# Spread gates stored in the order of the output stage's reads: short writes and long reads in a hybrid conv/HGRN2/PEER layer

## Chip, cores and metric

The kernel runs on one core of a Trainium2 chip. The metric is the device time of one execution in microseconds; smaller is better.

## What is computed

One decoder layer over 1024 tokens of 1024 features: a mixer (convolution and gated recurrence), then PEER, a retrieval over 128 x 128 single-neuron experts, and a final norm. The change lies in PEER:

```
s1, i1 = top_k(sc[:, :, 0], 16); s2, i2 = top_k(sc[:, :, 1], 16)     # 8 heads, 128 keys on each side
top_s, ci = top_k((s1[..., :, None] + s2[..., None, :]).reshape(t, 8, 256), 16)
experts = i1[ci // 16] * 128 + i2[ci % 16]
gate = softmax(top_s)
act = gelu(einsum('thkd,td->thk', u_tab[experts], xb))
y   = einsum('thk,thkd->td', gate * act, v_tab[experts])
h   = h + y;  out = rmsnorm(h)
```

## The kernel before

Tokens stand in 8 tiles of 128. For two of them (GATHERED) the chosen expert rows are fetched by indirect DMA and handled on VectorE. For the other six (DENSE, TD = 768 tokens) the kernel computes all 16384 experts densely: TensorE makes the activation of every expert for every token, the gates of the chosen ones are spread into a dense array that is zero elsewhere, and the product of both is multiplied with the whole value table. Experts are worked on as 128 columns of 128, an expert's place within a column being the partition.

**Activation stage** (`select_and_activate`, lines 1411 to 1980), 128 columns. For a column SP loads a 512 KB weight tile (`Ring.load`, L84), ScalarE splits it in a high part and a scaled copy (`Ring.high`, L89 and L90), GpSimd makes the low part (`Ring.low`, L95), TensorE does two units of 24 matmuls (L1605 to L1607), ScalarE applies the gelu (L1663) to `ge`, and SP writes it to `acts_dram` (L1570). Weight tiles alternate between two buffers, and SP issues the load for column s + 2 ahead of the activation write of column s (`pick`, L1566). The columns run in parts: 64 beside the top-k searches on VectorE (`pick`), 4 of lead, 48 in which the gates are spread (`spread`), 12 `alone`.

**Spreading.** For eight tokens at a time (an octet, two per column) VectorE builds one-hot matrices (L1923 to L1927), TensorE multiplies them (L1638), and ScalarE copies the result from PSUM into `tile` (two L1707 per octet). `tile` has two halves u of 32 tokens x 128 columns (16 KB a partition); a half is full after two columns, and SP then writes its 2 MB to `gates_dram` (L1578), 24 writes in all. ScalarE waits for the semaphore `g_st[u]` before it fills a half again (L1704). In `spread` ScalarE's order within a column is gelu, octet, gelu, octet, then L89 and L90 for the column after next. The rows of the weight table that the two other tiles need are fetched by GpSimd (L1758) on the software queue and used by VectorE (L1800), between the steps above.

**Output stage** (`combine`, L1983 on), 32 groups of CPG = 4 columns. SP loads a group's gates (`Head.load_gates`, L329, 1.5 MB) and activations (`Head.load_acts`, L333, 1.5 MB), and four value tiles of 512 KB (`Head.load_values`, L345); VectorE multiplies gates and activations (`weigh`, L317), ScalarE and GpSimd split values and weights (L2171, L2177; L2198, L2203), TensorE does 144 matmuls (L2152 to L2154), VectorE adds the result (L2320) and works on gathered rows (L2298) that GpSimd fetches (L2237). Gates of groups 0 and 1 come early, in the `alone` columns, in four pieces each (`Head.load_piece`, L340), after SP has waited for the last gates writes (L1589).

Each engine takes its instructions in order. SP issues all plain DMAs on one hardware queue; GpSimd issues the gathers on a software queue. Both queues run on the same 16 DMA engines.

`gates_dram` has the shape (24, 128, 4096): block b of 32 tokens, partition, and 128 columns x 32 tokens. `Head.__init__` gives the view of it by group that the reads use (L298).

Of the kernel before, what the change touches and what calls it, by code (L numbers as in the profile page):

```python
# [6 lines left out]
P = 128  # L7
# [19 lines left out]
TD = DENSE * P  # L27
DHALF = TD // 2
GT = 32
CPG = 4  # L30
GROUPS = NK // CPG
# [40 lines left out]
class Ring:  # L72
# [3 lines left out]
    def __init__(self, sems, label, buffers, base):  # L76
        self.wf, self.wh, self.wl = buffers
        self.w_in = [sems(f"{label}_in{s}") for s in range(2)]
        self.w_hi, self.w_lo = sems(f"{label}_hi"), sems(f"{label}_lo")
        self.base = base  # L80
# [204 lines left out]
class Head:  # L285
# [5 lines left out]
    def __init__(self, sems, scores, gates, acts, v_t, vf, share):  # L291
        flat = scores[:, :, :, :].rearrange("p a h n -> p (a h n)")
        size = CPG * TD
        at = flat.shape[1] - 4 * size
        self.vh = flat[:, 0:at].bitcast(BF16).rearrange("p (s c n) -> p s c n", s=2, c=CPG)
        self.gt = flat[:, at:at + 2 * size].rearrange("p (s b c t) -> p s b c t", s=2, c=CPG, t=GT)
        self.at = flat[:, at + 2 * size:at + 4 * size].rearrange("p (s c n) -> p s c n", s=2, c=CPG)
        self.gates = gates.rearrange("b p (g n) -> g p b n", g=GROUPS)  # L298
        self.acts = acts.rearrange("(g c) p n -> g p c n", g=GROUPS)
        self.v_t, self.vf = v_t, [vf[:, s, :] for s in range(2)]  # L300
        self.v_in = [sems(f"v_in{s}") for s in range(CPG)]
        self.g_in = [sems(f"gt_in{s}") for s in range(2)]
        self.a_in = [sems(f"at_in{s}") for s in range(2)]
        self.w_ok, self.w_hi, self.w_lo = (sems(n) for n in ("gw_ok", "gw_hi", "gw_lo"))


        self.ge_st = [sems(f"ge_st{s}") for s in range(2)]
        self.share = share
        self.w_first = [share[:, i * size // 2:(i + 1) * size // 2].bitcast(BF16).rearrange("p (c n) -> p c n", c=CPG)
                        for i in range(2)]  # L310
# [1094 lines left out]
def after(eng, sem, count):  # L1405

    if not (isinstance(count, int) and count <= 0):
        eng.wait_ge(sem, count)  # L1408


def select_and_activate(nc, ctx, sb, sems, psum, scores, ident, iota16, const_b, xh, xl, ring, u_t, gates, acts, rows,
# [73 lines left out]
    flat = scores[:, :, :, :].rearrange("p a h n -> p (a h n)")  # L1485
# [4 lines left out]
    tile = flat[:, at:at + 2 * NK * GT].rearrange("p (u c t) -> p u c t", u=2, c=NK)  # L1490
# [6 lines left out]
    g_st = [sems(f"g_st{s}") for s in range(2)]  # L1497
# [8 lines left out]
    def slots(eng, pick, lead, spread, between=None, unroll=None, few=None, last=None):  # L1506


        for j in range(PICK):
            pick(j, j % 2, 0, j)  # L1510
        for start, end, body in (((1, TB, pick),) if few is None else (
                (1, FEW_TURNS, few), (FEW_TURNS, ALL_TURNS, pick))):
            with eng.Fori(start, end) as n:
                for j in range(PICK):
                    body(PICK * n + j, j % 2, n, j)
        if between is not None:
            between()
        for j in range(LEAD):
            lead(PICKED + j, j % 2, j)
        for j in range(LOOP):  # L1520
            spread(FIRST_G + j, j % 2, 0, j)
        with eng.Fori(1, SPREAD // LOOP if last is None else SWITCH - 1) as n:
            for j in range(LOOP):
                spread(LOOP * n + (FIRST_G + j), j % 2, n, j)
        if last is not None:

            n = SWITCH - 1
            for j in range(LOOP):
                (spread if j < LOOP - 2 else last)(LOOP * n + (FIRST_G + j), j % 2, n, j)
            with eng.Fori(SWITCH, SPREAD // LOOP) as n:  # L1530
                for j in range(LOOP):
                    last(LOOP * n + (FIRST_G + j), j % 2, n, j)
        if unroll is not None:
            for j in range(ALONE):
                unroll(LAST_G + j, j % 2, j)
            return
        with eng.Fori(0, ALONE // LOOP - 1) as n:
            for j in range(LOOP):
                pick(LOOP * n + (LAST_G + j), j % 2, None, 2 * n + j // 2, j)
        for j in range(LOOP):  # L1540
            pick(NK - LOOP + j, j % 2, None, (ALONE - LOOP + j) // 2, j)
# [12 lines left out]
    def more(s):  # L1554

        return not (isinstance(s, int) and s >= NK - 2)

    with nc.Block() as blk:
        @blk.sync
        def _(sp):  # L1560
            def load(s, par):

                after(sp, u_lo, s - 1)
                ring.load(sp, par, u_t[ds(s, 1), :, :])

            def pick(s, par, n, j, slot=None):  # L1566
                if more(s):
                    load(s + 2, par)
                sp.wait_ge(a_ge, 2 * s + 2)
                sp.dma_start(acts[ds(s, 1), :, :].rearrange("a p n -> (a p) n"), ge[:, par, :]).then_inc(ge_st[par], 16)  # L1570

            def spread(s, par, n, j):
                pick(s, par, n, j)
                if j % 2 == 1:

                    u = j // 2
                    sp.wait_ge(g_ok, 16 * n + (8 * u + 8))
                    sp.dma_start(gates[ds(2 * n + u, 1), :, :].rearrange("a p n -> (a p) n"),  # L1578
                                 tile[:, u, :, :].rearrange("p c t -> p (c t)")).then_inc(g_st[u], 16)

            def alone(s, par, j):

                if j >= ALONE - 2:
                    sp.wait_ge(u_lo, s + 1)
                    head.load_values(sp, par, par)
                pick(s, par, None, j)
                if j == 1:
                    for u in range(2):
                        sp.wait_ge(g_st[u], 16 * (SPREAD // LOOP))  # L1589
                if 0 < j <= 2 * PIECES:  # L1590
                    head.load_piece(sp, (j - 1) // PIECES, (j - 1) % PIECES)

            sp.dma_start(xtok[0], normed[0, :, :]).then_inc(tok_in, 16)
            slots(sp, pick, lambda s, par, j: pick(s, par, None, j), spread, unroll=alone)

        @blk.tensor
# [850 lines left out]
```

## Time and profile before

| | |
|---|---|
| median of 3 runs | 2834.77 us (2832.07 to 2835.41) |
| span of the profiled execution | 2830.4 us |
| TensorE, VectorE, GpSimd, ScalarE busy | 97%, 77%, 58%, 39% of the span |
| DMA | 658.08 MB, mean 233 GB/s |
| gates writes | 24 of 2048 KB, median 9.2 us to landing |
| gates reads, activation reads | 30 each of 1536 KB, 16.4 and 19.8 us |

The trace is one execution recorded by the hardware profiler. Times are from the start of the span. PE is TensorE's matmuls, PEld its weight loads, DVE is VectorE, ACT ScalarE, POOL GpSimd, SP SyncE. PE's ends are modelled, since matmuls are pipelined. "Idle before <- X" says what ended an engine's idle time. A DMA packet is one contiguous piece; q1 is the queue of SP, q0 that of GpSimd. The DMA share is the mean busy share of the 16 DMA engines.

### The profile page before, as it was taken

How to read it: one execution, taken by the hardware profiler on the slowest of the kernel's cores; microseconds unless marked ns; L12 is line 12 of the kernel's file. 1: busy time of each engine (PE TensorE's matmuls, PEld its weight loads, DVE VectorE, ACT ScalarE, POOL GpSimd, SP SyncE). 2: the span in 40 equal slices, each digit the busy share in tenths (PEclk: the TensorE clock that was granted, in tenths of full speed). 3: DMA queues.
4: the chain of work that ended last, by engine and by line, in shares of the span. 5: the costliest groups of instructions: out<-in, count | busy, mean ns of one | idle time of the engine just before them, and what ended most of it. 6: DMA issues, size and time to landing. Idle time of an engine off the chain costs nothing. (4 is left out here: it accounts for less than half of the span.)

```text
span 2830.4 us, 47325 instructions
## 1 busy us (share of the span) xinstructions
PE 2757.7 (97%) x16000; PEld 1508.1 (53%) x16000; DVE 2169.3 (77%) x4268; ACT 1115.4 (39%) x1554; POOL 1628.8 (58%) x1485
## 2 busy tenths in 40 slices
PE   6999999999999999999999999999999999999998
PEld 3445754554666666656666665444444444444443
DVE  3998865322788999989999994777777777777778
ACT  4354554223444444446677664312211221222122
POOL 1331001111233444477777775888888898889884
PEclk9999999999999999999999999999999999999999
DMA  3231030111344555568888888899999999999995
GB/s 128 79 137 35 1 139 22 58 47 42 110 156 162 191 192 185 177 238 308 321 308 308 322 307 321 316 367 330 338 343 339 328 343 358 352 343 352 358 349 189
DMA packets 265252, 658.08 MB, mean 233 GB/s; under 512 B 17552, under 2 KB 116112, under 8 KB 261952
## 3 DMA queue, kind: packets, MB, share of 16 engines
q1 hardware_dynamic: 190992, 387.37, 38.2%
q0 software_dynamic: 74160, 269.52, 26.7%
q8 instruction: 45, 0.74, 0.1%
q14 instruction: 55, 0.45, 0.1%
HBM read 547.24 MB, written 110.10 MB: 232 GB/s over the span
## 5 line engine op out<-in xcount | busy, mean ns | idle before, releaser
L95 POOL TENSOR_TENSOR w_low<-w_ring,w_high 128x1024 f16<-128x1024 f32 x164 | 375.3, 2289 | 884.9 <-ACT w_ring L90 884.3
L1605 PE MATMUL psum<-region_y,w_high 128*128 128x384 f16 x2048 | 670.4, 327 | 10.8 <-issue 4.3
L1606 PE MATMUL psum<-region_y,w_high 128*128 128x384 f16 x2048 | 670.5, 327 | 0.0
L1607 PE MATMUL psum<-region_y,w_low 128*128 128x384 f16 x2048 | 670.4, 327 | 0.0
L2320 DVE TENSOR_TENSOR region_x<-region_x,psum 128x1024 f32<-128x1024 f32 x192 | 234.3, 1220 | 213.6 <-PE psum L2154 213.4
L2171 ACT ACTIVATE scores<-w_ring 128x1024 bf16<-128x1024 f32 x64 | 67.0, 1048 | 655.6 <-PE psum L2154 651.6
L2152 PE MATMUL psum<-scores,share 128*128 128x512 bf16 x752 | 286.0, 380 | 7.7 <-DVE region_x L2320 6.9
L2152 PE MATMUL psum<-scores,wh 128*128 128x512 bf16 x768 | 291.2, 379 | 1.4 <-POOL wl L2203 1.4
L2154 PE MATMUL psum<-scores,wl 128*128 128x512 bf16 x768 | 291.2, 379 | 0.0
L2153 PE MATMUL psum<-vl,wh 128*128 128x512 bf16 x768 | 291.2, 379 | 0.0
L1663 ACT ACTIVATE ge<-psum 128x384 f32<-128x384 f32 x256 | 124.9, 488 | 415.6 <-PE psum L1607 413.5
L2153 PE MATMUL psum<-vl,share 128*128 128x512 bf16 x752 | 285.9, 380 | 0.0
L2154 PE MATMUL psum<-scores,share 128*128 128x512 bf16 x752 | 285.9, 380 | 0.0
L1605 PEld LDWEIGHTS psum<-region_y,w_high 128*128 128x128 f16 x2048 | 200.7, 98 | 139.4 <-issue 13.8
L1607 PEld LDWEIGHTS psum<-region_y,w_low 128*128 128x128 f16 x2048 | 200.9, 98 | 134.0 <-issue 2.2
L1606 PEld LDWEIGHTS psum<-region_y,w_high 128*128 128x128 f16 x2048 | 200.8, 98 | 126.8 <-issue 2.1
L2298 DVE SCALAR_TENSOR_TENSOR psum<-region_y,weight,psum 128x1024 f32<-128x1024 f32 x176 | 226.4, 1286 | 11.3 <-DVE psum L2298 4.2
L89 ACT ACTIVATE w_high<-w_ring 128x1024 f16<-128x1024 f32 x164 | 172.8, 1054 | 86.5 <-DMA w_ring<-in_u_t_dram 66.3
L1707 ACT ACTIVATE scores<-psum 128x512 f32<-128x512 f32 x192 | 188.8, 1088 | 30.9 <-PE psum L1638 30.9
L2237 POOL DMA_INDIRECT region_y<-in_v_t_dram,step_rows x176 | 167.6, 952 | 48.7 <-issue 48.4
L90 ACT ACTIVATE w_ring<-w_ring 128x1024 f32<-128x1024 f32 x164 | 171.6, 1046 | 0.0
L1758 POOL DMA_INDIRECT scores<-in_u_rows_dram,u_step_rows x112 | 129.7, 1158 | 25.4 <-issue 18.8
(306 smaller groups left out, 5478.3 us busy)
## 6 DMA issues: line engine op xcount, KB each, us to landing
w_ring<-in_u_t_dram SPq DMA_DIRECT2D x128, 512.0 KB, 6.1
acts_dram<-ge SPq DMA_DIRECT2D x128, 384.0 KB, 4.8
gates_dram<-scores SPq DMA_DIRECT2D x24, 2048.0 KB, 9.2
scores<-gates_dram SPq DMA_DIRECT2D x30, 1536.0 KB, 16.4
scores<-acts_dram SPq DMA_DIRECT2D x30, 1536.0 KB, 19.8
w_ring<-in_v_t_dram SPq DMA_DIRECT2D x64, 512.0 KB, 11.0
more_v<-in_v_t_dram SPq DMA_DIRECT2D x64, 512.0 KB, 4.9
w_ring<-in_w_stream_dram SPq DMA_DIRECT2D x20, 512.0 KB, 3.5
```

The costliest lines, as they stand in the source:

```text
L89: act.activation(self.wh[:, s, :], self.wf[:, s, :], ACT.Copy, scale=WS)
L90: act.activation(self.wf[:, s, :], self.wf[:, s, :], ACT.Copy, scale=WS).then_inc(self.w_hi, 1)
L95: pool.tensor_tensor(self.wl[:, s, :], self.wf[:, s, :], self.wh[:, s, :], ALU.subtract).then_inc(self.w_lo, 1)
L1605: pe.matmul(a, uh[:, par, row], xh[:, n, cols], start=(n == 0), stop=False)
L1606: pe.matmul(a, uh[:, par, row], xl[:, n, cols], start=False, stop=False)
L1607: last = pe.matmul(a, ul[:, par, row], xh[:, n, cols], start=False, stop=(n == KC - 1))
L1707: act.activation(tile[:, u, :, at:at + 4].rearrange("p c t -> p t c"), psum[:, 4 + 2 * r + b, :].rearrange("p (t c) -> p t c", t=4), ACT.C ...
L2152: pe.matmul(a, wh[par][:, c, rows], vh[:, par, c, cols], start=(c == 0), stop=False)
L2153: pe.matmul(a, wh[par][:, c, rows], vl[:, par, c, cols], start=False, stop=False)
L2154: last = pe.matmul(a, wl[par][:, c, rows], vh[:, par, c, cols], start=False, stop=(c == CPG - 1))
L2298: dve.scalar_tensor_tensor(out=acc[tile], in0=row[j], scalar=weight[:, tile, ds(at, 1)], in1=acc[tile], op0=ALU.mult, op1=ALU.add).then_in ...
L2320: dve.tensor_tensor(a, a, banks, ALU.add).then_inc(y_ok, 1)
```

## The change

The array `gates_dram` keeps its size and its data; their order in it becomes group, partition, block of 32 tokens, then the group's 4 columns x 32 tokens. A group's gates of one partition are then 24 x 512 B = 12 KB in one piece. A block's gates of one partition, which were 16 KB in one piece, are now 32 pieces of 512 B, one in each group's part. The SBUF side of every transfer, all instructions, waits and the order of issues stay.

```
-        self.gates = gates.rearrange("b p (g n) -> g p b n", g=GROUPS)
+        flat = gates.rearrange("b p n -> (b p n)")
+        self.gates = flat.rearrange("(g p b n) -> g p b n", g=GROUPS, p=P, b=TD // GT)
+        self.gates_of = flat.rearrange("(g p b n) -> b p g n", g=GROUPS, p=P, b=TD // GT)
...
                     sp.wait_ge(g_ok, 16 * n + (8 * u + 8))
-                    sp.dma_start(gates[ds(2 * n + u, 1), :, :].rearrange("a p n -> (a p) n"),
-                                 tile[:, u, :, :].rearrange("p c t -> p (c t)")).then_inc(g_st[u], 16)
+                    sp.dma_start(head.gates_of[ds(2 * n + u, 1), :, :, :].rearrange("a p g n -> (a p) g n"),
+                                 tile[:, u, :, :].rearrange("p (g c) t -> p g (c t)", c=CPG)).then_inc(g_st[u], 16)
```

## Rows read from the trace of the kernel before

**Rows 1.** Busy us (x instructions) by stage; last TensorE's granted clock, DMA share, GB/s
```profile
1300.00:1700.00 400.00, 399.24 (x3318) 270.36 (x3317) 383.56 (x540) 277.95 (x334) 289.60 (x252) 1.00 0.82 312
1820.00:1900.00 80.00, 72.32 (x325) 31.91 (x324) 67.60 (x68) 20.93 (x24) 70.49 (x67) 0.96 1.01 363
1900.00:2300.00 400.00, 400.00 (x1855) 181.34 (x1854) 294.58 (x334) 88.56 (x102) 350.56 (x335) 1.00 0.96 337
2400.00:2700.00 300.00, 298.47 (x1378) 134.02 (x1377) 232.51 (x201) 64.08 (x74) 268.57 (x257) 1.00 0.98 350
```
**Rows 2.** Timeline of SP in the spread stage: start, duration, line, operation
```profile
1421.54 0.33 SPq L1578 DMA_DIRECT2D gates_dram<-scores  x1
1422.07 0.35 SPq L84 DMA_DIRECT2D w_ring<-in_u_t_dram  x1
1428.77 0.33 SPq L1570 DMA_DIRECT2D acts_dram<-ge  x1
1429.30 0.35 SPq L84 DMA_DIRECT2D w_ring<-in_u_t_dram  x1
...
1440.82 0.33 SPq L1578 DMA_DIRECT2D gates_dram<-scores  x1
...
1460.08 0.33 SPq L1578 DMA_DIRECT2D gates_dram<-scores  x1
```
**Rows 3.** Timeline of ScalarE, same turn; in brackets idle time and what ended it
```profile
1432.74 1.06 ACT L89 ACTIVATE w_high<-w_ring 128x1024 f16<-128x1024 f32 x1 [1.73 <-DMA w_ring<-in_u_t_dram]
1433.70 1.04 ACT L90 ACTIVATE w_ring<-w_ring 128x1024 f32<-128x1024 f32 x1
1434.65 0.47 ACT L1663 ACTIVATE ge<-psum 128x384 f32<-128x384 f32 x1
1435.02 1.95 ACT L1707 ACTIVATE scores<-psum 128x512 f32<-128x512 f32 x2
```
**Rows 4.** Timeline of GpSimd, same turn
```profile
1434.82 2.92 POOL L95 TENSOR_TENSOR w_low<-w_ring,w_high 128x1024 f16<-128x1024 f32 x1 [3.58 <-ACT w_ring L90]
```
**Rows 5.** Timeline of TensorE, first matmul of the next column
```profile
1438.46 0.32 PE L1605 MATMUL psum<-region_y,w_high 128*128 128x384 f16 x1
```
**Rows 6.** Waits, 1260 to 1720 us: total us, times, longest
```profile
ACT w_high L89 <- DMA w_ring<-in_u_t_dram: 44.8, 22, 3.4
...
PE psum L1605 <- POOL w_low L95: 0.8, 1, 0.8
```
**Rows 7.** DMA queues (packets, MB, share of 16 engines): 1425.5-1427.5; 1832-1838; 1886.6-1887.9; 2135.5-2136.5
```profile
q1 hardware_dynamic: 45, 0.74, 94.7%
...
q0 software_dynamic: 441, 1.58, 67.7%
q1 hardware_dynamic: 1233, 0.63, 37.6%
...
q1 hardware_dynamic: 316, 0.16, 64.9%
...
q1 hardware_dynamic: 346, 0.18, 70.4%
```
**Rows 8.** Landings: gates writes 1300-1700, gates reads 1830-2760; last, SP's L333 (ns)
```profile
DMA to landing us min/median/max: 7.4/8.9/10.3
...
DMA to landing us min/median/max: 14.9/16.4/25.3
...
L333 SPq DMA_DIRECT2D scores<-acts_dram x30: 6440/10029/19663, 1822.8 to 2728.2; - x30
```
**Rows 9.** Timeline of GpSimd, gathers issued beside the write and the load
```profile
1428.58 1.25 POOL L1758 DMA_INDIRECT tk_work<-in_u_rows_dram,u_step_rows  x1 [0.15 <-issue]
1430.14 1.10 POOL L1758 DMA_INDIRECT tk_work<-in_u_rows_dram,u_step_rows  x1 [0.31 <-issue]
```
**Rows 10.** Waits in the output stage, 1820 to 2800 us
```profile
ACT scores L2171 <- PE psum L2154: 651.6, 30, 22.5
DVE region_x L2320 <- PE psum L2154: 212.0, 151, 2.8
...
ACT scores L2171 <- DMA w_ring<-in_v_t_dram: 3.9, 1, 3.9
ACT scores L2171 <- DMA more_v<-in_v_t_dram: 3.1, 2, 2.5
```
**Rows 11.** Gates writes (count, first to last start); timeline of SP after the last
```profile
L1578 SPq DMA_DIRECT2D gates_dram<-scores x24: 332/332/343, 1267.3 to 1711.5; - x24
...
1726.36 0.34 SPq L1570 DMA_DIRECT2D acts_dram<-ge  x1
```

## Prediction, made before the changed kernel was run

> **What bounds the kernel now.** I read first the busy times by stage [rows 1]. In the spread stage (the 48 columns in which the gates are spread and written, about 1267 to 1726 us) TensorE is busy 399.2 of 400 us at full clock; in the output stage it is busy 400.0 of 400 in its first half and 298.5 of 300 in its second, with one gap of 7.7 us just after its start (1820 to 1900). So TensorE sets the time of both stages that the change touches, and nothing gained off TensorE can be worth more than its idle time. The question is only whether the change makes TensorE wait.
>
> Second view: the order of SP's issues in the spread stage [rows 2]. A turn is two columns: the gates writes start at 1421.54, 1440.82 and 1460.08, so a turn is 19.27 us, and there are 24 writes [rows 11]. Half a microsecond behind each write, on the same queue, stands the load of the weight tile that TensorE needs one and a half columns later.
>
> Third view: what happens when that load lands [rows 3 to 5]. ScalarE starts L89 at 1432.74, after an idle time of 1.73 us that the DMA ended: 11.2 us after the write was issued at 1421.54. L89 and L90 take 1.9 us, GpSimd's L95 runs from 1434.82 to 1437.74, and TensorE begins the column that needs it at 1438.46. This path has 0.7 us to spare. It is not a single case: ScalarE waited for that DMA 22 times in the stage, 44.8 us in all, while TensorE lost 0.8 us to it once [rows 6]. The load behind the gates write is the one thing in the stage that is nearly late.
>
> **The change, part by part.** (a) Each of the 24 writes keeps its 2 MB, but a partition's 16 KB row becomes 32 pieces of 512 B, 12 KB times 128 apart in memory: 4096 pieces in place of 128. (b) Each of the 30 reads keeps its 1.5 MB and has 12 KB rows in place of 24 pieces of 512 B; the 8 early pieces have 3 KB rows. (c) Nothing else moves; no instruction and no wait is added.
>
> Cost of the write in the DMA engines. With 16 KB rows, hardware-queue packets took 94.7% of 16 engines x 2 us for 45 packets: 673 ns each, so 128 / 16 x 673 ns = 5.4 us. For 512 B pieces the trace of before has only reads. Beside backlogged gathers 1233 packets took 37.6% of 96 us: 29.3 ns each; 4096 / 16 x 29.3 ns = 7.5 us is the lower end. But alone on the engines these pieces did not come at that pace: 316 in 1.3 us (243 per us) with the engines 64.9% busy, and 346 in 1.0 us at 70.4% [rows 7]. Something ahead of the engines supplied only 243 to 346 per us: 16.9 to 11.8 us for 4096. I take the middle, 295 per us, 13.9 us, since the write mostly meets engines that are not backlogged. The far end is the read's whole landing: 14.9 us at least for 3072 pieces [rows 8], by 4/3 19.9 us, against 8.9 us for a write now, so 11.0 us more.
>
> The Trainium skill (DMA: Bandwidth & Descriptors, Specifications) gives 512 B as the smallest transfer that runs at line rate. By that the write would stay as it is and this sum would be zero. The trace disagrees even in engine time alone: 512 B in 29.3 ns is 17.5 GB/s per engine, 16 KB in 673 ns is 24.3 [rows 7].
>
> The load behind it. L, from the write's issue to ScalarE's start, is now 11.2 us. It grows by 13.9 - 5.4 = 8.5 us. Against that, two gathers that now share the engines with the load (issued at 1428.58 and 1430.14 [rows 9]) will mostly be through before it: 256 packets / 16 x 147 ns (from the 441 packets of the software queue in 67.7% of 96 us [rows 7]) = 2.4 us. L = 11.2 + 8.5 - 2.4 = 17.3 us.
>
> What a turn then takes. ScalarE is in order: behind the load it must do L89 and L90, a gelu, the octet's two copies, another gelu and two copies before SP may issue the next write: 1.9 + 0.4 + 1.95 + 0.4 + 1.95 us [rows 3], with 0.1 for the semaphore 6.7 us. So a turn is the longer of 19.27 us and L + 6.7. Now: 17.9, hidden. After: 24.0, which is 4.7 us more per turn. TensorE follows: its column starts after L + 1.9 + 2.9 and stands idle for the same 4.7 us. 24 turns x 4.7 us = 113 us.
>
> Queues behind it. SP, ScalarE and GpSimd wait in order. SP: in the output stage the acts load issued right behind a 512 B gates read held SP for 6.4 to 19.7 us [rows 8], so SP will be held likewise at the weight load behind the write, and the acts write and the next column's load, now issued 7.2 and 7.8 us after the gates write [rows 2], go out later. The turn of 24 us leaves both time, so I add nothing; if not, the second column of a turn waits too (in the far end of the range). ScalarE's own wait for a tile half that is still being written: it reuses that half one turn later, and the write lands at about 8.9 + 8.5 = 17.4 us, inside 24. GpSimd's gathers behind L95 shift with the turn; VectorE is busy 383.6 of 400 us [rows 1] and gets slack. Cost 0 for these. SP waits for the last write before the first early piece; that write was issued at 1711.5 and the wait is reached near 1726.7, behind the acts write of 1726.36 [rows 11]: landing at 17.4 us after its issue it would hold SP for some 2 us, taken as 0.
>
> The output stage. Reads with 12 KB rows free the engines of 3072 x (29.3 ns - 21 ns at the 16 KB rate) / 16 = 1.6 us per group of 31 us, and SP's long hold at the acts load goes. Who waits for it? In 1820 to 2800 us [rows 10] ScalarE waits 651.6 us and VectorE 212.0 us for TensorE; no wait for a gates or acts load is among them, only 7.0 us for value tiles at the start. Gain taken as 0. Its bounds: TensorE's idle time, 7.7 us at the start and 1.5 us in 300 later, so at most about 11 us; and a small loss, if 12 KB rows crowd out the gathers: not seen, since each gather is issued a group ahead.
>
> Sum: 2830.4 us (the profiled span) + 113 = 2943.4. The median of the three runs is 4.4 us above that span, so 2948 us.
>
> **Rivals.** (1) *The engines are the limit, not the supply.* 7.5 us for the write, no relief from the gathers: L = 11.2 + 2.1 = 13.3, a turn of 20.0, +0.7 x 24 = 17 us: 2852. For it: where a backlog stood ahead, pieces took 29.3 ns. Against: both stretches in which they were alone. (2) *Slower still.* The write grows by 11.0 us and nothing is relieved: L = 22.2, a turn of 28.9, +9.6 x 24 = 231 us: 3066. For it: these are writes, whose price at 512 B no row shows. (3) *No change.* The write's pieces are as quick as the long rows, or the growth stays under 19.27 - 6.7 - 11.2 = 1.4 us: 2835. This is what the skill's 512 B figure would give. Against: 5.4 to 7.5 us is already over 1.4. (4) *Faster.* Place: the output stage's start and its second half, where TensorE is idle 7.7 and 1.5 us; price -9 to -11 us, 2825; it decides only where the write grows by under 1.4 us, as in (3), and the idle time hangs on the gates reads. Against: rows 10 show none of it waiting for them. That the change doesn't do what it says is excluded: the diff alters the two address patterns and nothing else.
>
> **How the numbers follow.** A measurement of this kernel tells about 0.2% (5.7 us) from no change. Supply-limited write (346 to 243 pieces per us: L of 15.2 to 20.3, turns of 21.9 to 27.0, +63 to +186 us: 2898 to 3021): 0.55. Rival (1) and up to +60: 0.18. Rival (2), over +186: 0.13. Rival (3): 0.08. Rival (4): 0.06. The range of 8 in 10 reaches from 2850, leaving out (3) and (4), to 3040, leaving out most of (2). Slower 0.86, same 0.08, faster 0.06.
>
> **What the next profile would show.** If right: gates writes landing in 14 to 18 us in place of 8.9; writes 23 to 25 us apart; ScalarE's wait for the weight load grown from 44.8 to some 150 us, about 7 us at every second column; TensorE idle 4 to 5 us per turn, named L1605 waiting for GpSimd's L95; SP held several us at the load behind the write; the alone columns and the output stage as before; and gates reads landing well under 16.4 us without effect. I am wrong in size if the writes land in under 12 us, wrong in mechanism if they land late and the turn stays at 19.3 us (the load is then not held behind them), and wrong in sign if the spread stage keeps its length and the output stage's start gets shorter.

## The result: slower by 46 us, and the profile after

| | before | changed |
|---|---|---|
| median | 2834.1 us (4 runs) | 2880.2 us (4 runs, 2875.4 to 2893.0) |
| ratio, 95% interval | | 1.018 (1.0166 to 1.0194) |
| span of the profiled execution | 2830.4 us | 2891.2 us |

The sign was right, the size was not: 113 us were forecast, 46 measured (61 in the profiled execution, the slowest of the four). The ratio and its interval are worked out from the single runs; the quotient of the two medians is 1.016. The changed kernel's lines are two further down (L84, L89, L90, L95 stay; L1578 is L1580, L329 is L331).

Where the 61 us lie can be read from SP's timeline. The first gates write starts at 1267.3 before and 1267.9 after, the last at 1711.5 [rows 11] and at 1767.3:

```profile
1767.29 0.38 SPq L1580 DMA_DIRECT2D gates_dram<-scores  x1
```

The 23 turns between them took 444.2 us before and 499.4 after, 55.2 more (19.3 and 21.7 us each). From the last write to the end it was 1118.9 and 1123.9, 5.0 more: behind the last write TensorE waits 6.5 us for GpSimd's L95 where it waited 3.1. So everything is lost in the spread stage and at the load behind its last write. By stages (columns as in rows 1), the changed kernel:

```profile
1268.00:1767.00 499.00, 460.74 (x3680) 305.31 (x3679) 405.62 (x597) 302.87 (x369) 304.57 (x275) 0.97 0.82 278
1883.00:2880.00 997.00, 983.41 (x4467) 445.49 (x4560) 766.14 (x755) 223.48 (x265) 864.44 (x829) 1.00 0.91 336
```

TensorE, busy 399.2 of 400 us before [rows 1], is idle 38 of 499 and its granted clock averages 0.97 of 2.4 GHz, with stretches at 1.2 GHz after idle time (0.50 from 1550.1 to 1553.5 us, after an idle time of 4.3 us; 34 us of the stage in all). In the output stage the DMA share is lower (0.91; the 997 us from 1822.4 on had 0.95 before), as the long reads should have it. From the stage's first gates read to the end it is 1008 us in both.

One turn with a stall, SP's timeline, then ScalarE's, GpSimd's and TensorE's (compare rows 2 to 5):

```profile
1572.65 0.38 SPq L1580 DMA_DIRECT2D gates_dram<-scores  x1
1573.23 7.91 SPq L84 DMA_DIRECT2D w_ring<-in_u_t_dram  x1
1581.41 0.64 SPq L1572 DMA_DIRECT2D acts_dram<-ge  x1
1582.24 0.35 SPq L84 DMA_DIRECT2D w_ring<-in_u_t_dram  x1
...
1594.65 0.38 SPq L1580 DMA_DIRECT2D gates_dram<-scores  x1
```

```profile
1588.13 1.06 ACT L89 ACTIVATE w_high<-w_ring 128x1024 f16<-128x1024 f32 x1 [6.01 <-DMA w_ring<-in_u_t_dram]
```

```profile
1590.21 2.34 POOL L95 TENSOR_TENSOR w_low<-w_ring,w_high 128x1024 f16<-128x1024 f32 x1 [7.86 <-ACT w_ring L90]
```

```profile
1592.81 0.33 PE L1607 MATMUL psum<-region_y,w_high 128*128 128x384 f16 x1 [3.08 <-ACT ge L1665]
```

The load behind the write reaches ScalarE 15.5 us after the write was issued (11.2 before), GpSimd's part ends at 1592.55 and TensorE starts right behind it, after 3 us of idle time. (The profile names ScalarE's gelu L1665, which ended at 1592.64 and stands behind L89 and L90 in ScalarE's order; so both waits hang on the same load.) The next write goes out 6.5 us after ScalarE's start. SP is held 7.9 us at the load. The waits between 1260 and 1800 us (total us, times, longest), against rows 6:

```profile
ACT w_high L89 <- DMA w_ring<-in_u_t_dram: 107.7, 24, 9.3
...
PEld psum L1607 <- ACT ge L1665: 36.1, 11, 6.2
PE psum L1607 <- POOL w_low L95: 33.7, 11, 6.5
```

And the landings of the page of the changed kernel (the gates writes took 9.2 us before, the gates reads 16.4):

```profile
gates_dram<-scores SPq DMA_DIRECT2D x24, 2048.0 KB, 12.0
scores<-gates_dram SPq DMA_DIRECT2D x30, 1536.0 KB, 9.5
```

The write lands 3 us later, not 8.5. That is the main difference between forecast and result; a second one, of the other sign, is the relief of 2.4 us that the forecast expected of the gathers (see below).

### The profile page after: what moved, and what is told of

It is laid out like the page before. It is cut to its first block and busy times, and to the rows that moved or that the text cites. A ratio compares the mean times of both kernels' runs of the same rounds, so it can differ in the third digit from the quotient of the medians.

```text
span 2891.2 us, 47201 instructions
## 1 busy us (share of the span) xinstructions
PE 2774.6 (96%) x15904; PEld 1513.9 (52%) x16000; DVE 2151.5 (74%) x4268; ACT 1110.4 (38%) x1554; POOL 1617.1 (56%) x1485
## 5 line engine op out<-in xcount | busy, mean ns | idle before, releaser
L95 POOL TENSOR_TENSOR w_low<-w_ring,w_high 128x1024 f16<-128x1024 f32 x164 | 367.2, 2239 | 955.4 <-ACT w_ring L90 954.9
L1665 ACT ACTIVATE ge<-psum 128x384 f32<-128x384 f32 x256 | 125.3, 490 | 432.2 <-PE psum L1609 431.2
L2154 PE MATMUL psum<-scores,share 128*128 128x512 bf16 x737 | 280.3, 380 | 8.3 <-DVE region_x L2322 6.5
L2154 PE MATMUL psum<-scores,wh 128*128 128x512 bf16 x752 | 285.1, 379 | 2.0 <-POOL wl L2205 1.2
L2155 PE MATMUL psum<-vl,wh 128*128 128x512 bf16 x752 | 285.0, 379 | 0.8
L2156 PE MATMUL psum<-scores,wl 128*128 128x512 bf16 x752 | 285.0, 379 | 0.8
L2156 PE MATMUL psum<-scores,share 128*128 128x512 bf16 x736 | 279.7, 380 | 0.8
L2155 PE MATMUL psum<-vl,share 128*128 128x512 bf16 x736 | 279.7, 380 | 0.8
L89 ACT ACTIVATE w_high<-w_ring 128x1024 f16<-128x1024 f32 x164 | 173.0, 1055 | 139.7 <-DMA w_ring<-in_u_t_dram 119.4
L90 ACT ACTIVATE w_ring<-w_ring 128x1024 f32<-128x1024 f32 x164 | 171.8, 1047 | 0.0
## 6 DMA issues: line engine op xcount, KB each, us to landing
scores<-acts_dram SPq DMA_DIRECT2D x30, 1536.0 KB, 17.4
```

The lines of the kernel that those rows point to most:

```text
L89: act.activation(self.wh[:, s, :], self.wf[:, s, :], ACT.Copy, scale=WS)
L90: act.activation(self.wf[:, s, :], self.wf[:, s, :], ACT.Copy, scale=WS).then_inc(self.w_hi, 1)
L95: pool.tensor_tensor(self.wl[:, s, :], self.wf[:, s, :], self.wh[:, s, :], ALU.subtract).then_inc(self.w_lo, 1)
L2154: pe.matmul(a, wh[par][:, c, rows], vh[:, par, c, cols], start=(c == 0), stop=False)
L2155: pe.matmul(a, wh[par][:, c, rows], vl[:, par, c, cols], start=False, stop=False)
L2156: last = pe.matmul(a, wl[par][:, c, rows], vh[:, par, c, cols], start=False, stop=(c == CPG - 1))
```

## Experiments

All are compared with runs of the kernel before on the same chip: median 2832.4 us for the first four runs, 2830.9 us for the other four. The theory after the result: short writes move at the pace of the DMA engines and land 3 us later than long ones, and the loss is that time ahead of one load. Rivals: the queue supplies short pieces slowly (as I had predicted); short pieces do harm of their own; the long reads give something back.

### b1: pieces alone

A kernel with DMAs only, each waited for (condensed; `old_g` is the old layout by group, `new_b` and `new_g` the changed one by block and by group):

```
for b in range(24): go(gates[b], src)             # 16 KB rows
for i in range(4):  go(new_b[5 * i + 1], s_b)      # write, 4096 x 512 B, changed layout
for i in range(4):  go(old_g[7 * i + 2], s_g)      # write, 3072 x 512 B, old layout
for i in range(4):  go(d_b, new_b[5 * i + 2])      # read, 4096 x 512 B, changed layout
for i in range(4):  go(d_g, old_g[7 * i + 3])      # read, 3072 x 512 B, old layout
for i in range(4):  go(d_g, new_g[7 * i + 4])      # read, 12 KB rows
```

> Nothing of the layer is computed here: the kernel only issues DMAs one at a time on SP's queue, each waited for, and writes zeros. In order: 24 long gates writes (16 KB rows), 4 short writes in the changed layout (4096 pieces of 512 B), 4 short writes in the old layout by group (3072 pieces of 512 B), 4 reads of 4096 pieces of 512 B from the changed layout, 4 reads of 3072 pieces of 512 B as the old output stage reads them, 4 reads with 12 KB rows. Theory (the DMA engines set the pace of a short write, and only reads of scattered 512 B are supplied slowly): short writes of 4096 pieces move at 500 to 600 pieces per us, some 7.5 us of packets and 9 to 11 us to landing, in both layouts by count; short reads move at 240 to 350 per us. Rival of the prediction (the queue supplies 512 B pieces at 243 to 346 per us whatever their direction): short writes take 12 to 17 us of packets. The 4 reads of the changed layout tell direction from pitch: if they are as slow as the old reads it is the direction, if as quick as the writes it was the old layout's 16 KB and 2 MB pitch.

SP's queue (packets, MB, share of 16 engines) in stretches that lie inside one transfer: 7 to 10 us long writes; 158 to 163 short writes; 221 to 226 short reads of the changed layout; 258 to 263 short reads of the old layout; 257.8 to 259.3 their slowest part.

```profile
q1 hardware_dynamic: 80, 1.31, 103.6%
...
q1 hardware_dynamic: 2833, 1.45, 102.1%
...
q1 hardware_dynamic: 2934, 1.50, 117.9%
...
q1 hardware_dynamic: 2192, 1.11, 85.1%
...
q1 hardware_dynamic: 506, 0.26, 86.0%
```

Short writes run at 2833 / 5 = 567 pieces per us with the engines full: 28.8 ns each (102.1% of 16 x 5 us over 2833). From the first packet's start to the last one's end a write of 4096 pieces took 7.4 us in the trace, one with long rows 5.1 (128 / 16 x 621 ns is 5.0): 2.3 to 2.4 us more. To landing it was the same 2.4 us more, 8.7 against 6.3:

```profile
gates_dram<-src SPq DMA_DIRECT2D x1, 2048.0 KB, 8.7
...
gates_dram<-src SPq DMA_DIRECT2D x1, 2048.0 KB, 6.3
```

(The 4.47 us in the expectations of e6 and e7 are the time to the start of the last packet and leave out its 0.62 us; so these two put more ahead of the load than they meant to.) The queue therefore supplies at least 567 per us, and the rival is out. The changed kernel's own trace says so too: where its write had the engines to itself, from 1576 to 1578 us, 1348 pieces started in 2 us, 674 per us.

```profile
q1 hardware_dynamic: 1348, 0.69, 113.7%
```

Short reads of the changed layout are as quick (587 per us). Only short reads of the old layout, 16 KB and 2 MB apart, are slower, 438 per us, and each has a dip, 506 / 1.5 = 337 per us, with the engines not full. Short writes to those same places took 5.54 us for 3072, 555 per us, so it needs both, that pitch and reading. The two stretches of rows 7 from which I had taken the supply (243 and 346 per us) lie 2 to 3 us behind the issue of such reads, in their first half, as three of the four dips of b1 do.

### e1 and e4: the weight load ahead of the gates write

```
             def spread(s, par, n, j):
-                pick(s, par, n, j)
+                first = isinstance(n, int) and n == 0 and j == 0
+                pick(s, par, n, j, loads=(j % 2 == 1 or first))
                 if j % 2 == 1:
+                    load(s + 3, 1 - par)
                     u = j // 2
                     sp.wait_ge(g_ok, 16 * n + (8 * u + 8))
```

(`pick` loads only where `loads` is set; the first of the `alone` columns leaves its load out too.) The same edit was made in the changed kernel (e1) and in the kernel before (e4).

> The changed kernel, with one move: in the spread columns SP issues the weight load for the second next column ahead of the gates write in place of just behind it (it is already free to go then). Theory (the whole loss is that one load standing behind the write): the load lands some 6 us after its issue, ScalarE's wait for it goes to nearly nothing, a turn is 19.3 us again, and the time is that of the kernel before within 0.2% (2834, 2828 to 2840). Rival (the short write takes DMA engine time or memory time from everything, so order does not matter): most of the 46 us stays, 2865 or more.

Measured e1: 2829.6 us, ratio 0.9986 (0.9977 to 0.9995). All of the 46 us is gone, and 3 to 4 us more (by the medians and by the ratio), with the short writes in place; they still take 12.5 us to land.

> The kernel before (long writes, short reads) with the same move of the weight load ahead of the gates write. If the small gain of the changed kernel with that move (ratio 0.9986) comes from the order alone, this one gains the same: 2830, within 2 us of it, since TensorE is the bound of a turn in both. If the long reads add something of their own, this one stays 3 us or more above it. The layouts should no longer differ at all: the load lands some 5 us after its issue in both.

Measured e4: 2827.6 us, ratio 0.9987 (0.9978 to 0.9996), the same gain as e1. The layouts make no difference once the load goes first, and the 0.13% is the order's. It answers to a small stall of the kernel before: at the last load behind a write TensorE waited 3.1 us for L95, and in e4 its idle time in 1700 to 1740 us is 0.3 us; the stages of e4 read

```profile
1267.00:1710.90 443.90, 443.90 (x3687) 300.63 (x3686) 422.34 (x596) 307.71 (x369) 313.06 (x276) 1.00 0.85 314
1700.00:1740.00 40.00, 39.69 (x266) 24.43 (x265) 17.07 (x27) 18.09 (x25) 23.02 (x29) 1.00 0.92 329
```

The waits of e1 between 1260 and 1700 us have this left of ScalarE's wait for the load:

```profile
ACT w_high L89 <- DMA w_ring<-in_u_t_dram: 0.2, 1, 0.2
```

### e2: long writes and long reads

```
-                    sp.dma_start(head.gates_of[ds(2 * n + u, 1), :, :, :].rearrange("a p g n -> (a p) g n"),
-                                 tile[:, u, :, :].rearrange("p (g c) t -> p g (c t)", c=CPG)).then_inc(g_st[u], 16)
+                    sp.dma_start(gates[ds(2 * n + u, 1), :, :].rearrange("a p n -> (a p) n"),
+                                 tile[:, u, :, :].rearrange("p c t -> p (c t)")).then_inc(g_st[u], 16)
```

> Long gates writes as before and long gates reads as in the change; the two layouts then don't agree, so the gates that the output stage reads are in the wrong order; all work is done. It gives what the long reads alone are worth. Theory: nothing waits for the gates reads, so 2834 within 0.2%. Rival (the long reads give something back in the output stage, which the change's loss hides): 2820 to 2828.

Measured: 2831.7 us, ratio 0.9997 (0.9988 to 1.0007). The long reads alone are worth nothing that can be measured.

### e5: short writes and short reads

```
-        self.gates = flat.rearrange("(g p b n) -> g p b n", g=GROUPS, p=P, b=TD // GT)
+        self.gates = gates.rearrange("b p (g n) -> g p b n", g=GROUPS)
```

> Short gates writes as in the change, short gates reads as before; the layouts don't agree, so the gates reach the output stage in the wrong order; all work is done. Theory (all of the loss is from the writes): the changed kernel's time, 2880 (2872 to 2890). Rival (the long reads win back a part): 4 us or more above the changed kernel.

Measured: 2882.5 us (2871.9 to 2887.4), ratio 1.0188 (1.0172 to 1.0203), the changed kernel's 1.018 within the two intervals. The loss is the writes'.

### e3: pieces of 1 KB

The two views are shown; the reads and the write index them accordingly.

```
-        self.gates = flat.rearrange("(g p b n) -> g p b n", g=GROUPS, p=P, b=TD // GT)
-        self.gates_of = flat.rearrange("(g p b n) -> b p g n", g=GROUPS, p=P, b=TD // GT)
+        self.gates = flat.rearrange("(h p b e n) -> h e p b n", h=GROUPS // 2, p=P, b=TD // GT, e=2)
+        self.gates_of = flat.rearrange("(h p b m) -> b p h m", h=GROUPS // 2, p=P, b=TD // GT)
```

> The gates are stored for two groups together: a write has 2048 pieces of 1 KB, a read again has 3072 pieces of 512 B (in pairs of pieces 1 KB apart). Theory: at engine pace a 1 KB piece takes about 45 ns (between 29 ns for 512 B and 160 ns for 4 KB), 2048/16 x 45 = 5.8 us against 5.4 for long rows, so the load lands under 1 us later than before, which is inside the 1.4 us to spare: 2834 to 2842. Rival (pieces are supplied at 243 to 346 per us): 2048 pieces take 6 to 8.4 us, up to 3 us more per turn, 2850 to 2880. Rival (what counts is the time of the sum of both queues): about half of the changed kernel's loss, 2857.

Measured: 2839.1 us, ratio 1.0033 (1.0023 to 1.0043), inside what the theory gave (2834 to 2842); the loss is a seventh of the changed kernel's by the medians, a fifth by the ratios. The load reached ScalarE 12.3 us after the write in the mean of 23 turns (11.4 before), and a turn took 19.4 us: nearly all of that still hides. Of the 6 us that the profiled execution lost, 2.6 lie in the turns and 3.4 behind the last write.

### e6 and e7: more time ahead of the load, without short pieces

The kernel before, with one more write between gates write and load (MORE is 1192 elements of a row in e6, 2640 in e7; ScalarE and SP wait for both writes; `gates_dram` is twice as large, and the reads use its first half; these lines are left out here):

```
+                    sp.dma_start(gates[ds(2 * n + (u + TD // GT), 1), :, 0:MORE].rearrange("a p n -> (a p) n"),
+                                 tile[:, u, :, :].rearrange("p c t -> p (c t)")[:, 0:MORE]).then_inc(g_st[u], 16)
```

> The kernel before, layouts untouched, with one more DMA between the gates write and the weight load: 4.8 KB of each row are written once more to a place that nobody reads, 0.6 MB in long rows, 1.3 us of packets by the 4.47 us that 2 MB took alone. No short piece is written. Theory (what counts is the DMA time that stands ahead of the load, and some 1.1 to 1.4 us are to spare): the load lands 1.3 us later, L 12.8, turns of 19.3 to 19.7, a loss of 0 to 10 us: 2832 to 2842. Rival (pieces of 512 B do harm of their own, by memory or by crowding): as before, 2832.

Measured e6: 2845.8 us, ratio 1.0051 (1.0035 to 1.0066), 4 us over what the theory gave. The mean turn was 19.63 us (first write 1267.80, last 1719.32, 23 turns), 7 us in all; L was 13.0 us in the mean. The other 6 us of the profiled execution are a stall behind the last write. The second write's packets took 203 ns each in the trace's mean, 8 to an engine: 1.6 us, which is what L grew by (11.4 to 13.0).

> The same with 10.6 KB of each row, 1.35 MB, 2.9 us of packets, which is what the short pieces add to a write alone on the engines (7.35 against 4.47 us). Theory: L grows by 2.9 to 3.3 us to about 14.5, a turn is L + 6.5 or TensorE's own at a lower granted clock, 21 to 21.7 us; 24 turns x 1.7 to 2.4 and a stall at the end: 2875 (2862 to 2888), the loss of the changed kernel without any short piece. Rival (the short pieces themselves do the harm): under 2850.

Measured e7: 2890.4 us, ratio 1.0202 (1.0186 to 1.0218), 2 us past the upper bound. Turns of 21.6 us (1267.41 to 1763.54), L of 15.0 us: close to the changed kernel's 21.7 and 14.8, without a short piece. The second write's packets took 451 ns each, 3.6 us, and L grew by 3.6. That is more than the 2.4 us that the short pieces add alone, so e7 does not match the changed kernel in packet time; it shows that the time ahead of the load goes into L, and that a turn follows L whatever makes it long. SP's timeline and ScalarE's (lines one further down, L90 is L89):

```profile
1721.14 0.33 SPq L1579 DMA_DIRECT2D gates_dram<-scores  x1
1721.67 0.33 SPq L1581 DMA_DIRECT2D gates_dram<-scores  x1
1722.55 0.56 SPq L85 DMA_DIRECT2D w_ring<-in_u_t_dram  x1
...
1742.42 0.33 SPq L1579 DMA_DIRECT2D gates_dram<-scores  x1
```

```profile
1735.90 1.06 ACT L90 ACTIVATE w_high<-w_ring 128x1024 f16<-128x1024 f32 x1 [4.95 <-DMA w_ring<-in_u_t_dram]
```

SP is not held here (0.56 us at the load, 7.9 in the changed kernel), and yet a turn is as long for its L: the next write follows ScalarE's start by 6.5 us, as in the changed kernel. So that hold costs nothing of its own that can be seen.

Put together, for the mean of 23 turns (L from the write's issue to ScalarE's start, read off the two timelines). L, turn and span are of the profiled execution, which was the slowest of the changed kernel's four and the fastest of e5's; the ratio is of all runs.

| kernel | L, us | turn, us | profiled span, us | ratio |
|---|---|---|---|---|
| before | 11.4 | 19.3 | 2830.4 | 1 |
| e3, 1 KB pieces | 12.3 | 19.4 | 2836.4 | 1.003 |
| e6, 1.6 us more | 13.0 | 19.6 | 2844.6 | 1.005 |
| e5, short writes and reads | 14.3 | 20.9 | 2870.1 | 1.019 |
| changed | 14.8 | 21.7 | 2891.2 | 1.018 |
| e7, 3.6 us more | 15.0 | 21.6 | 2890.0 | 1.020 |

## Why the prediction was right or wrong

**What bounds the kernel, and the thin slack.** Right. TensorE is the bound, and the load half a microsecond behind the gates write was the one thing nearly late. e1 shows it: moved ahead, it takes the whole loss with it.

**The write's cost.** Here the prediction failed, at "13.9 us of packets". The step put the supply of pieces at 243 to 346 per us from two stretches in which short *reads* were alone, and laid it on the queue. b1 shows that the queue supplies at least 567 per us, so that the write alone takes 7.4 us; the slow stretches are a property of reading 512 B at the old layout's pitch, which the write does not share. The lower end (29.3 ns, 7.5 us) was the right one: 28.8 ns and 7.4 us. I had even the row for it, a backlog of reads at 29.3 ns, and set it aside because the write would meet engines that are not backlogged. What I had not done was to ask whether the stretches that were slow had anything but their size in common with the write.

**The load behind it, L.** By the forecast L would go from 11.2 to 17.3; it went from 11.4 to 14.8. Of the growth of 3.3 us, 2.4 is the write's own, as b1 has it alone. So rival (1), the engines as the limit, had the mechanism and nearly the write's growth (2.1). It gave 17 us where 46 were measured, because its L of 13.3 was 1.5 too small: L was read from one turn, 0.2 us under the mean, 0.3 is missing in the write's growth, and some 0.9 us comes from the gathers, which it put at nothing.

The second wrong term of the forecast is the gathers' relief of 2.4 us. The gathers do not wait for the short write to end; they slow it down. From 1297 to 1299 us, with both queues busy, the trace has

```profile
q0 software_dynamic: 174, 0.65, 90.3%
q1 hardware_dynamic: 176, 0.09, 15.1%
```

as many packets of the one as of the other, but with some 4 KB in a gather's and 512 B in the write's. Before, from 1425.5 to 1427.5 us, it was 35 packets of gathers with 17.4% of the engines' time beside 45 long rows [rows 7] with 94.7%. Counted over the 24 writes in the traces' packets, 296 gather packets started within a short write in the mean and 117 within a long one, 1.9 us more of each engine's time; within the load behind it they fell only from 121 to 96. With the write's growth put right and the relief kept, the forecast's own sum would have been 11.2 + 2.4 - 2.4 = 11.2 us, no loss at all: the two errors worked against each other, and the sign came out right with the help of the larger one. No run separates the gathers' part, since none of the layer left them out; that they are the 0.9 us is argued from these counts.

L swings between 12.8 and 18.0 us from turn to turn. In the turn of 18.0 us 459 packets of gathers started while the write was under way (1483.7 to 1497.2), in the turn shown above 204 (1575.6 to 1583.6).

**The turn, L + 6.7.** Right where the load leads: in the turn shown above the next write follows ScalarE's start by 6.5 us. With the mean L it gives 21.3 us; the mean turn is 21.7. The rest is in turns like 1550.89 to 1572.65, where L was 13.7 and the turn 21.8: there TensorE itself was late, restarted after the last stall at a granted clock below full and busy all the time:

```profile
1550.00:1560.00 10.00, 10.00 (x67) 6.05 (x65) 4.83 (x9) 5.01 (x7) 8.96 (x9) 0.83 0.87 267
```

I had not counted the clock. Its part is bounded by the turns: in the changed kernel's profile the next write followed ScalarE's start by 6.4 to 6.6 us where the load led, and by more in eight of the 23 turns, 9.5 us more in all. So the lower clock can hold at most some 9.5 of the 55 us there; the same sum is 1.5 us for e5 and 0.6 for e7, which lost 36 and 52 us in their turns. Among the single runs the longer ones also have the lower mean clock (2875.4 us at 0.991, 2893.0 at 0.984; e5 2871.9 at 0.992, 2887.4 at 0.986). Which of the two drives the other from run to run was not separated.

**The queues behind the write.** Right: SP's hold of 5 to 9 us at the load came as described and cost nothing that can be seen: e7 has the loss without it, and e5 has the hold (4.9 to 7.8 us) and no more time in a turn than L + 6.6.

**The output stage, taken as 0.** Right, by e2 (0.9997) and e5 (1.0188 against 1.018). Reads that land in 9.5 us in place of 16.4 had nobody who waited for them, and their gain in DMA share bought nothing. Rivals (3) and (4) fall as well: 3.3 us more is past the slack. The slack itself is now measured: 0.9 us later (e3) costs 0.3%, 1.6 us (e6) 0.5%, 2.9 to 3.6 us (e5, changed, e7) 1.8 to 2.0%. The prediction had two figures for it, 0.7 us at L95 and 1.4 us in the turn; e6, whose turns of L 12.9 took 19.5 us, speaks for some 1.3. It is softer than a threshold, since the single turns scatter around the mean.

**The 512 B figure.** The Trainium skill (DMA: Bandwidth & Descriptors, Specifications) has 512 B as the smallest transfer at line rate. b1 disagrees: at 28.8 ns for 512 B the 16 engines move 284 GB/s, at 621 ns for 16 KB they move 422 GB/s.

## What to carry to other kernels

Before trading short writes for long reads, find out who waits for each, and what is queued behind each: the reads here had no waiter, and the write had a load behind it with about a microsecond to spare. What short pieces cost alone is not all that they cost beside another queue: a second queue's larger packets can take most of the engines' time while both are busy (90% in the stretch shown). Where a queue carries bulk and urgent transfers, issue the urgent one first; moving one load by one place was worth more (0.13% below the kernel before) than either layout, and with it the layouts no longer differ (e1, e4). A rate read from one stretch of a trace belongs to its direction and its addresses; before it is lent to another transfer, look for a second stretch that shares only the size.

## What the runs showed of the hardware

- A 512 B piece took 28.8 ns of a DMA engine in writing, a 16 KB row 621 ns (103.6% of 16 x 3 us over 80), so 32 pieces cost 1.5 times the long row. To landing, alone, a 2 MB write took 8.7 us in short pieces and 6.3 in long rows.
- Beside gathers of 4 KB packets a write of 512 B pieces got as many packets as they did (176 and 174 in 2 us) and 15.1% of the engines' time against their 90.3%.
- Reads of 512 B at a pitch of 16 KB and 2 MB ran at 438 pieces per us with a dip to 337; reads of the changed layout, 12 KB and 1.5 MB apart, ran at 587, writes at either near 560. Why the dip comes is open.
- A DMA issued on SP right behind one of 3072 to 4096 pieces held SP for 5 to 20 us (7.9 in the turn shown), but not behind long rows of as many bytes (0.35 us). Behind 2048 pieces of 1 KB (e3) it was 1.2 to 5.0 us.
